# Hybrid decoder layer on one core: waits and first steps moved at five joins between stages

## What is computed

```python
def decoder_layer(x, nsa_fn, ...):
    xn = rmsnorm(x, g_mix)
    q, kvc, kvs, kvw, gt, mu, mv, mo, mi, mf = split(xn @ w_in)
    o_cmp, o_sel, o_win, ... = nsa_fn(q, kvc, kvs, kvw)        # three attention branches
    o_nsa = rmsnorm(gates * (o_cmp, o_sel, o_win), g_nsa)
    o_m, ... = mlstm_mixer(mu, mv, mo, mi, mf, ...)            # 4 heads of 128
    h = x + concatenate([o_m, o_nsa]) @ w_out
    up = causal_dwconv(rmsnorm(h, g_ffn) @ w_up)
    a, g = split(up)
    return h + (silu(g) * a) @ w_down

def compress_blocks(rows, pe, w1, w2):                         # per 32 rows, keys and values apart
    blk = rows.reshape(b, nb, 32, h, d) + pe
    return silu(blk.reshape(b, nb, h, 32 * d) @ w1) @ w2
```

## Time and profile before

| | us |
|---|---|
| median of 3 runs | 1076.31 (1075.5 to 1076.8) |
| the profiled execution, device time | 1076.65 |
| the profiled execution, span of the trace | 1074.9 |
| TensorE busy in it | 1018.1 (95%) |
| VectorE, ScalarE, GpSimd busy | 612.9, 404.1, 152.7 |
| projection ends, batch 0 of the compression starts | 182.5, 184.2 |
| heads start, samples start | 290.0, 380.0 |
| prompt attention starts (its first exponent) | 470.3 |

### The profile page before, as it was taken

How to read it: one execution, slowest core, us unless ns; L and a number is a source line. 1 busy time by engine, 2 the same in 40 slices (tenths; PEclk the granted TensorE clock), 3 DMA queues, 4 the chain that set the end, 5 groups by cost and what they waited for, 6 DMA issues and landing times.

```text
span 1074.9 us, 19288 instructions
## 1 busy us (share of the span) xinstructions
PE 1018.1 (95%) x7776; PEld 917.0 (85%) x7776; DVE 612.9 (57%) x1305; ACT 404.1 (38%) x759; POOL 152.7 (14%) x207
## 2 busy tenths in 40 slices
PE   4999998999999979989899999999999999999996
PEld 4999998999866647665559999999999999999996
DVE  3736753444267656677957336676767677932222
ACT  4223422333143346448764333333333333621212
POOL 3200020330112221016740000000000000000000
PEclk9999999999999989999999999999999999999999
DMA  6561162553511165334012222222222222332322
GB/s 185 186 180 40 56 205 79 209 184 138 240 44 42 42 259 198 122 110 141 2 59 100 78 81 82 81 81 81 81 81 81 81 81 56 91 93 65 96 54 88
DMA packets 82074, 114.26 MB, mean 106 GB/s; under 512 B 10086, under 2 KB 72648, under 8 KB 79263
## 3 DMA queue, kind: packets, MB, share of 16 engines
q1 hardware_dynamic: 75247, 70.60, 21.2%
q0 software_dynamic: 6768, 42.84, 10.8%
HBM read 103.33 MB, written 13.59 MB: 109 GB/s over the span
## 4 chain that ended last, share of the span: by engine, by line
PE 83%; DVE 8%; DMA 3%; ACT 2%; issue 2%; POOL 1%; SPq 0%; DVEq 0%; ACTq 0%
PE banks L1619 14%; PE banks L1617 11%; PE banks L1659 6%; PE banks L1074 5%; PE banks L1129 5%; PE banks L1658 5%; PE banks L1077 4%; PE banks L1078 4%; PE banks L1572 3%; PE banks L1113 2%; PE banks L1571 2%; PE banks L1329 2%; PE banks L1318 2%; PE banks L1690 2%; PE banks L1393 1%
## 5 line engine op out<-in xcount | busy, mean ns | idle before, releaser
L1619 PE MATMUL banks<-xnT_r,RB_r 128*128 128x320 f32 x352 | 109.8, 312 | 0.0
L1619 PE MATMUL banks<-xnT_r,ring_r 128*128 128x320 f32 x352 | 109.4, 311 | 0.0
L1617 PE MATMUL banks<-xnT_r,RB_r 128*128 128x256 f32 x352 | 103.3, 294 | 0.0
L1617 PE MATMUL banks<-xnT_r,ring_r 128*128 128x256 f32 x352 | 98.9, 281 | 0.0
L1619 PE MATMUL banks<-RC_r,RB_r 128*128 128x320 f32 x264 | 82.3, 312 | 0.0
L1129 PE MATMUL banks<-RA,RB 128*128 128x128 f32 (+1 forms) x512 | 71.8, 282 | 2.9 <-DVE RA L1948 1.5
L1617 PE MATMUL banks<-RC_r,RB_r 128*128 128x256 f32 x264 | 74.3, 281 | 0.0
L2345 DVE TENSOR_TENSOR ring_r<-ring,RB_r 128x2048 fp32r<-128x2048 f32 x22 | 49.4, 2289 | 38.1 <-ACT RB_r L886 38.1
L1129 PEld LDWEIGHTS banks<-RA,RB 128*128 128x128 f32 x512 | 65.0, 191 | 4.4 <-ACT RA L668 2.3
L1617 PEld LDWEIGHTS banks<-xnT_r,RB_r 128*128 128x128 f32 x352 | 67.0, 190 | 1.2
L1617 PEld LDWEIGHTS banks<-xnT_r,ring_r 128*128 128x128 f32 x352 | 67.5, 192 | 0.0
(11 more groups left out here) (651 smaller groups left out, 2928.2 us busy)
## 6 DMA issues: line engine op xcount, KB each, us to landing
ring<-in_w_up_dram SPq DMA_DIRECT2D x22, 1024.0 KB
ring<-in_w_down_dram SPq DMA_DIRECT2D x8, 1408.0 KB, 7.0
ring<-in_w_in_dram SPq DMA_DIRECT2D x10, 1024.0 KB, 6.2
RB<-in_state_win_dram SPq DMA_DIRECT2D x8, 512.0 KB
out_win_s_dram<-in_state_win_dram POOLq DMA_DIRECT2D x1, 4032.0 KB
xsp<-RC SPq DMA_DIRECT2D x1, 2304.0 KB, 9.0
xT<-xsp SPq DMA_DIRECT2D x1, 2304.0 KB, 12.9
RA<-in_x_prompt_dram SPq DMA_DIRECT2D x4, 512.0 KB, 5.6
```

The lines of the kernel that those rows point to most:

```text
L1617: t.matmul(ps[4 + par][:, w * UA:(w + 1) * UA], wk[:, w, k, c], x[:, 0:UA], skip_group_check=True, **first)
L1619: last = t.matmul(ps[2 * par + w][:, 0:UB], wk[:, w, k, c], x[:, UA:T], **on)
```

## The change

1. **Projection to compression.** The two `hsum` matmuls stand ahead of job 37. The first half of batch 0's keys is packed ahead of job 37's eviction, into `first`, a free piece of RB; the second half behind the eviction. Turn 0 of batch 0 waits only for job 36's eviction. Batch 0 leaves TensorE's loop, which is now two rounds of batches 1 to 4, with batch 5 behind it. In batch 0 VectorE's `pack_next` stands behind turns 4 and 6 and the copy of the keys.
2. **Compression to heads.** The wait for `c_kcd` stands behind the four transposes.
3. **In each head.** ScalarE signals after mkT and again after mk, and TensorE waits for the second only ahead of the matmuls into `ps[4]`. `kbd` is built behind W.
4. **Last head's gate.** It goes from GpSimd to VectorE, behind `mix_head(3)`.
5. **Samples, pair 0.** ScalarE's `keys(0, 2)` stands ahead of `exp_cmp(1)`.

```diff
+        first = RB[:, 7016:8040].rearrange("p (h j d) -> p h j d", h=2, j=8)
...
             pool.dma_start(O["n_s"][0].rearrange("b h d -> b (h d)"), nbh).then_inc(S("m_stored"), 16)
-            gated(MH - 1)
             g.memset(Vbd, 0.0).then_inc(S("p_pool"), 1)
...
-                a.activation(mkT[:, 0:SEQ], ps[2][:, :], ACT.Copy, scale=KSCALE)
+                a.activation(mkT[:, 0:SEQ], ps[2][:, :], ACT.Copy, scale=KSCALE).then_inc(S("m_proja"), 1)
...
                 if p < 4:
                     keys(p, 1)
+                if p == 0:
+                    keys(p, 2)
                 if p < 3:
                     exp_cmp(p + 1)
-                if p < 4:
+                if 0 < p < 4:
                     keys(p, 2)
...
                 last.then_inc(S("job"), 1)
+                if n == len(jobs) - 2:
+                    pe.wait_ge(S("setup_dve"), 3)
+                    for kvi in range(2):
+                        last = t.matmul(ps[5][:, kvi:kvi + 1], hsum[:, kvi, :], ones[:, 0:1], start=True, stop=True)
+                    last.then_inc(S("cols_made"), 1)
...
+            pe.wait_ge(S("ev_act"), evac[-2][0])
+            pe.wait_ge(S("ev_dve"), evac[-2][1])
+            pe.wait_ge(S("setup_dve"), 4)
+            turn(0, 0, True)
+            pe.wait_ge(S("ev_act"), evac[-1][0])
+            pe.wait_ge(S("ev_dve"), evac[-1][1])
+            turn(0, 1, True)
+            pe.wait_ge(S("w1_in"), 4 * 16)
             hidden(0, 0, False)
-            with pe.Fori(0, NB // 2 - 1) as it:
-                for s in range(2):
-                    compress_pe(it * 2 + s, s)
+            compress_pe(0, 0, at_start=True)
+            with pe.Fori(0, 2) as it:
+                compress_pe(it * 2 + 1, 1)
+                compress_pe(it * 2 + 2, 0)
+            compress_pe(NB - 3, 1)
...
-            pe.wait_ge(S("c_kcd"), 2 + 2 * 8)
             pe.wait_ge(S("m_rcol"), 1)
             for k in range(MH):
                 last = t.transpose(ps[5][0:27, k * P:(k + 1) * P], mcg[:, k, :], ident[:])
             last.then_inc(S("m_cols"), 1)
 
+            pe.wait_ge(S("c_kcd"), 2 + 2 * 8)
             pe.wait_ge(S("pool_step"), 6)
...
-                pe.wait_ge(S("m_proja"), h + 1)
+                pe.wait_ge(S("m_proja"), 2 * h + 1)
                 for j in range(4):
+                    if j == 2:
+                        pe.wait_ge(S("m_proja"), 2 * h + 2)
...
+                if n == len(jobs) - 2:
+                    dve.wait_ge(S("rows_in0"), 16)
+                    src = ring[:, 0, :].rearrange("p (j k h d) -> p j k h d", j=16, k=2, h=2)
+                    v.tensor_copy(first, src[:, 0:8, 0, :, :].rearrange("p j h d -> p h j d")).then_inc(S("setup_dve"), 1)
...
                 values()
-                pack_next(b, 1 - s, seen)
+                if not at_start:
+                    pack_next(b, 1 - s, seen)
                 turned_cols(b, 4)
                 turned_cols(b, 6)
                 keys_of(it, s)
+                if at_start:
+                    pack_next(b, 1 - s, seen)
                 turned_cols(b + 1, 0)
...
-            dve.wait_ge(S("rows_in0"), 16)
-            pack(0, 0, 0)
+            late = ring[:, 0, :].rearrange("p (j k h d) -> p j k h d", j=16, k=2, h=2)[:, 8:16, 0, :, :]
+            v.tensor_copy(packed[:, 0, :].rearrange("p (h j d) -> p h j d", h=2, j=16)[:, :, 8:16, :],
+                          late.rearrange("p j h d -> p h j d")).then_inc(S("c_packed"), 1)
...
+                if h == MH - 1:
+                    dve.wait_ge(S("m_mixd"), MH)
+                    dve.wait_ge(S("m_mix"), MH - 1)
+                    v.tensor_tensor(xnT[:, h, :], xnT[:, h, :], moT[:, h, :], ALU.mult).then_inc(S("m_mix"), 1)
...
-                v.scalar_tensor_tensor(out=kbd[0:NSMP, :, :], in0=bmask.unsqueeze(2).to_broadcast([NSMP, NB, P]), scalar=0.0,
-                                       in1=mk[0:NSMP, 4:5, :].to_broadcast([NSMP, NB, P]), op0=ALU.is_equal,
-                                       op1=ALU.mult)
...
                                 ALU.mult).then_inc(S("m_w"), 1)
+                v.scalar_tensor_tensor(out=kbd[0:NSMP, :, :], in0=bmask.unsqueeze(2).to_broadcast([NSMP, NB, P]), scalar=0.0,
+                                       in1=mk[0:NSMP, 4:5, :].to_broadcast([NSMP, NB, P]), op0=ALU.is_equal,
+                                       op1=ALU.mult)
```

26 lines of the change are left out of this document (9 added, 17 removed).

## The result

The changed kernel took 1065.0 us in the median of four runs (1061.9 to 1067.8), the kernel before 1076.6 beside it (1075.5 to 1077.0): a ratio of 0.989, 95% interval 0.9865 to 0.9919. A second set of five runs gave 1066.8 us and 0.990 (0.9883 to 0.9917). The forecast was 1068.2, in a range of 1064.8 to 1071.8: the direction and the range held, and 1.4 to 3.2 us more came than forecast. The profiled execution of the changed kernel is the slowest of its four (span 1066.0 against 1074.9 before), so the two traces show 8.9 us of gain.

A forecast was written before the change was run, and what follows sets the result against it. TensorE, busy nearly all the span, was taken as the bound, so only its idle and slow time could be won: 2.6 + 0.6 + 1.55 + 0 + 3.4 = 8.15 us, giving 1068.2 us, range 1064.8 to 1071.8.

The forecast's parts named there:

- Projection to compression: Job 37 into batch 0: earlier turns and later `pack_next` remove TensorE waits, 2.6 us won (1.9 to 3.0).
- The low end of this join: Batch 0: TensorE's clock falls to about half all the same, so only 1.9 us is won.
- Compression to heads: Start of the heads: four transposes run during VectorE's last copies, shortening a 0.9 us wait by 0.6.
- Heads: All heads: earlier mkT signal and later `kbd` shorten waits for scores and W, 1.55 us won (0.8 to 2.1).
- The term for head 1: Head 1: the earlier mkT signal shortens the wait ahead of its scores, 0.25 us won.
- Last gate: VectorE ahead of clearing `pcd`: the gate fits into idle time, 0 us won, up to 0.8 lost.
- Samples: Pair 0: VectorE's two idle times, 2.19 and 1.19 us, both go; 3.4 us won.
- The low end, 2.2: Samples, pair 0: VectorE's second idle time stays, so only 2.2 us is won.
- more waits for DMA: No-change rival: idle time only moves to DMA waits, 6 us and more of them; 1075 to 1076.3 us, chance 0.05.
- More: Rival: slow clock stretches in heads 0 and 2 go too; with one gone 1065 to 1066.5 us, chance 0.14.
- Slower by clock: Rival: TensorE spends more time at half clock, likely in the prompt attention; about 1079 us, chance 0.03.
- second sign of being wrong: Anywhere in the changed kernel's trace: a slow stretch of clock in a place that had none.

The follow-up runs named there:

- next_early: The changed kernel with `pack_next` of batch 1 back in its old place, ahead of turn 4's copy: 1071.4 us, 0.9939 of the kernel before.
- seam_a: The kernel before with part 1 of the change alone (projection to compression, batch 0): 1071.1 us, 0.9948 of the kernel before.
- mix_silu: The changed kernel with project(0)'s first half ahead of the small transposes and one table load in the compression: 1060.0 us, 0.9852 of the kernel before.
- silu_once: The changed kernel with ScalarE's compression loop unrolled and a one-column SiLU ahead, for one table load: 1062.4 us, 0.9875 of the kernel before.
- the control: The kernel before, unedited, run against other runs of itself: 1076.3 us, ratio 0.9988.
- heads_both: The kernel before with both edits of the heads (signal behind mkT, `kbd` behind W): 1074.6 us, 0.998 of the kernel before.
- samples_e: The kernel before with part 5 alone (`keys(0, 2)` ahead of `exp_cmp(1)`): 1071.9 us, 0.995 of the kernel before.

## Why the prediction was right, and where it was off

- **What bounds the kernel: right.** Waits of TensorE that went came off the span, through the 670 us behind the samples, whose length is 670.9 to 673.5 for any kernel and follows mostly the slow time in it: 670.9 and 671.2 with 3.4 us, 671.7 to 672.9 with 6.8, 673.5 twice with 10.2.
- **Projection to compression: forecast 2.6 (1.9 to 3.0), shown 2.2 to 3.4.** All its marks held: piece 1 at 4.29 behind job 37's eviction (forecast 4.4), no wait ahead of piece 4, 0.53 ahead of piece 5. `pack_next` began at 194.62 (195.1) without a wait. The spare time towards the gather was put at 1.1; next_early's gather landed 10.92 behind the eviction, which is 193.4 here, so it is 1.2. What was off is the typical size. The six traces with the old join have 25.2 to 26.4 us, 25.9 on average, so the gain is 2.9: the 3.0 of the working, which set new turns at full clock against an old row at half clock; 2.6 allowed for a slow stretch that did not come. How much of the 2.9 is clock can't be told exactly; a stretch of 3.4 us there is worth about 1.5.
- **The low end of this join, 1.9, fell.** Batch 0 has no slow stretch in seam_a, in the two traces of the changed kernel, the two with project(0) moved, and mix_silu: its turns run at full clock in six traces. One came where TensorE idled 4.30 us in it (next_early), and one where it idled 1.00 (silu_once), though the same 1.00 brought none in mix_silu. The rule of the Trainium skill, TensorE: Matmul & The Clock Gate, section Part 4: PE-mode transpose, that transposes don't count as busy in the way of other matmuls, was taken to mean that the slow stretch would stay; it did not. The rule itself isn't refuted by that, as full matmuls stand between the turns of batch 0 from turn 1 on.
- **Compression to heads: forecast 0.6 (0.3 to 0.9), shown 0.7.** The compression, with no slow stretch in it, went from 90.28 (seam_a) to 89.55. This part wasn't run by itself: the 0.9 of waiting is gone, and the transposes stand where the mark said. Against a trace whose slow stretch began earlier (91.98 in the control) it is 2.1 to 2.4.
- **Heads: forecast 1.55 (0.8 to 2.1), shown 2.0 at full clock.** From W to W it took 19.39, 19.4 (20.63 less the 1.2 for the states) and 19.39 us where no slow stretch lay in the old heads; 18.88, 18.88 and 18.41 in silu_once, whose heads have none. Per head 0.5, 0.5 and 1.0, forecast 0.25, 0.5 and 0.8. CT and `kbd` are never waited for, as forecast; W still waits 1.30 in head 3, where about 1 was. The term for head 1 failed, 0.25 taken from what was left of the waits: the scores began 0.46 sooner behind the turned states (0.49 us behind them, 0.95 before), and the gain needed `kbd` late as well, which the forecast had not seen. That head 2's wait for the states stays was wrong: it is in no trace of the changed kernel or of those built on it. It was in three of seven before, 0.6 us on average, and the sum had nothing for it.
- **Last gate: 0, right** as far as the trace shows: 0.98 us of waiting for the store is left behind it, and from head 3's W to the samples' first score it is 12.09 us with the gate on either engine (heads_both, changed). It wasn't run by itself.
- **Samples: forecast 3.4, shown 3.5** (22.7 on average in six traces, 19.2 in the eight others), and by both idle times of VectorE. TensorE's wait of 3.43 has become 0.32 and 0.90. The low end, 2.2, fell, though part of the second idle time was TensorE at half clock (samples_e above).
- **Rivals.** No case of more waits for DMA came. "More" came in part: not since the stretches named there went (that at 288 stayed, head 2's stayed in most traces), but since the kernel before typically has more slow time than its first profile. "Slower by clock" fell; the clock went the other way, 0.981 to 0.987 or more. The prediction's second sign of being wrong, a slow stretch in a place that had none, did come: 3.4 us in head 1, which cost 1.6. It isn't of the change's making alone, since seam_a and samples_e have one there with the old heads. Nor does it follow on idle time, as the prediction had it of the known ones: TensorE's list has no wait between 301.11 and 362.32 of the changed kernel's trace, and both slow stretches of heads 1 and 2 (322.5, 343.0) lie in between.
- **The sum.** 2.9 + 0.7 + 2.0 + 3.5 is 9.1, where the forecast had 8.15; 2.9 and 3.5 hold the slow stretches that went with the old joins, 0.7 and 2.0 are at like clock. The medians gave 10.8 to 11.5. Of the last 2 us, 0.6 may be the states' wait and the rest slow stretches elsewhere, such as the 2.1 to 2.4 at the end of the compression against the control. That is argued from traces, and with a control 1.3 us from itself it can't be given to a part of the change.

## What to carry to other kernels

When two waits lie in a row on one chain, price the pair: either edit of the heads alone brought nothing in head 1, both 0.5. A step that is moved up must have what it reads: the join with batch 0 gained 2.9 us only because the pack that waits for the gather was moved down, and with it in its place was 2.2 us longer than the old one, in its one trace. And cut several traces at the same instructions before giving a difference of medians to an edit, since start and clock move a run by several us without any.

## What the runs showed of the hardware

- **The clock takes its toll in pieces of 3.4 us or twice or three times that** (the last 20 us left aside), at 0.50 to 0.53, at places that differ from run to run of one program; a piece in which TensorE is at work costs 1.6 us (W's matmuls of head 1, from W to W 18.88 to 20.48). The same program had medians of 1061.2 and 1064.6 in two sets. One place recurs: in eleven of the fourteen traces a stretch begins within 0.9 us of the start of W's matmuls of head 1, right behind the four short matmuls of the spread (4 partitions), with at most 0.44 us of waiting in that head ahead of it. Whether the spread is the cause was not tried.
- **The loss can be more than small.** The Trainium skill, TensorE: Matmul & The Clock Gate, section What's actually happening, puts the penalty of the ramp, the first slow matmuls of a busy time, below 1% of a typical span. The stretches here lie in the middle of work, and the kernel before has a mean clock of 0.981, 38 us of 1075 at half clock in the control, in a kernel whose TensorE is busy 95% of the time: up to 19 us, or 1.8%, if all of it lay at work.
- **A late operand costs more than the matmul's own wait shows.** Each round of ScalarE's loop cost TensorE 0.70 us of waits in its rows and 1.23 in time (batch 2 took 12.95 us with the two table loads and 11.72 without), probably since the weight loads wait as well.
